# Moving eight of the 32 branch-gate tiles from between the prompt steps into the sampled attention

## What is computed

```python
qa, ka, va, ra, lra, qb, kb, vb, fb, ga, gb = split(h @ w_in)      # ga, gb: (tokens, 2048) each
o_gla = gla_chunked(qa, ka, va, log_a, s0)                         # gated linear attention
# FoX, prompt: causal softmax attention with a forget bias, 8 heads of 128
# FoX, sample: q (4 tokens) against cache_k[page_table], cache_v[page_table], 1024 rows, 8 heads, each of 8 sequences
u_a = (rmsnorm(o_gla) * silu(ra)) @ w_up_a
u_b = o_fox @ w_up_b
merged = sigmoid(ga) * u_a + sigmoid(gb) * u_b
x = x + gt1 * (merged @ w_out)
# then a mixture of experts with 16 experts, and a final norm
```

## Time and profile before

| | us |
|---|---|
| median of 3 runs | 2014.64 |
| lowest and highest | 2011.6 to 2017.98 |
| the profiled execution's own time | 2012.6 |
| its span, first to last instruction | 2011.0 |

### The profile page before, as it was taken

The page is one execution under the profiler, slowest core; times in us unless marked ns, Lnnn a source line. Parts: engine busy times, 40 slices in busy tenths (PEclk is TensorE's granted clock), DMA queues, the critical chain, the costliest instruction groups (busy, mean ns, idle before and its releaser), DMA issues.

```text
span 2011.0 us, 28008 instructions
## 1 busy us (share of the span) xinstructions
PE 1792.2 (89%) x11118; PEld 1123.2 (56%) x11118; DVE 536.1 (27%) x1145; ACT 210.2 (10%) x403; POOL 154.1 (8%) x266
## 2 busy tenths in 40 slices
PE   6589999999998999999667899998699898999998
PEld 3055666666666777777545677776333333333334
DVE  2020000000017643332665311102423322232223
ACT  2010000000001110111223110001200001000102
POOL 1011021111110000150000000000100000000000
PEclk9889999999999999999778899999799999998998
DMA  9997676775705433543799985324299999999991
GB/s 359 420 359 273 238 284 222 266 290 192 272 22 172 156 96 106 179 158 104 297 410 410 365 307 195 119 94 168 68 366 393 408 383 395 409 392 403 369 395 47
DMA packets 142972, 530.89 MB, mean 264 GB/s; under 512 B 17637, under 2 KB 54667, under 8 KB 116123
## 3 DMA queue, kind: packets, MB, share of 16 engines
q1 hardware_dynamic: 117876, 433.50, 56.3%
q0 software_dynamic: 16704, 95.96, 13.6%
q10 hardware_dynamic: 8336, 0.66, 0.3%
HBM read 510.94 MB, written 19.15 MB: 264 GB/s over the span
## 4 chain that ended last, share of the span: by engine, by line
PE 74%; DMA 12%; DVE 5%; issue 4%; SPq 3%; DVEq 1%; ACT 1%; POOLq 0%; POOL 0%; ACTq 0%
PE ps L610 71%; DMA ring<-in_w_up_e_dram 4%; DMA ring<-in_cache_k_dram 3%; DMA ring<-in_w_ada_dram 3%; DMA xT<-in_w_ada_dram 2%; PE ps L620 2%; SPq L377 1%; DVE ring L1701 1%; SPq L383 1%; DVE z L1354 1%; DVE ring L1351 1%; DVE z L1345 1%; DMA z<-in_x_sample_dram 0%; DVEq L1976 0%; DVE ring L1441 0%
## 5 line engine op out<-in xcount | busy, mean ns | idle before, releaser
L610 PE MATMUL ps<-hT,ring 128*128 128x288 f32 x2560 | 649.1, 412 | 8.3 <-ACT hT L1169 6.3
L610 PEld LDWEIGHTS ps<-hT,ring 128*128 128x128 f32 x2560 | 483.5, 192 | 178.6 <-issue 51.1
L610 PE MATMUL ps<-ring,work 128*64 128x512 f32 (+1 forms) x1280 | 279.4, 636 | 37.9 <-DMA ring<-in_w_ada_dram 26.8
L610 PE MATMUL ps<-ring,z 32*32 32x256 f32 (+3 forms) x3744 | 227.5, 438 | 69.3 <-DVE ring L1701 53.4
L610 PE MATMUL ps<-z,ring 128*128 128x288 f32 (+1 forms) x1040 | 257.7, 408 | 5.7 <-PE ps L610 3.1
L1354 DVE COPY z<-ps 128x256 f32<-128x256 f32 (+7 forms) x98 | 64.4, 660 | 708.5 <-PE ps L610 678.2
L610 PEld LDWEIGHTS ps<-z,ring 128*128 128x128 f32 x1040 | 197.6, 191 | 64.0 <-issue 8.0
L610 PEld LDWEIGHTS ps<-ring,z 32*32 32x32 f32 (+3 forms) x3744 | 113.3, 121 | 171.2 <-issue 164.0
L610 PEld LDWEIGHTS ps<-ring,work 128*64 128x64 f32 (+1 forms) x1280 | 78.3, 135 | 204.1 <-issue 163.2
L1169 ACT ACTIVATE z<-ps 128x512 f32<-128x512 f32 (+4 forms) x108 | 60.4, 601 | 923.0 <-PE ps L610 909.2
L1351 DVE SCALAR_TENSOR_TENSOR xT<-ps,modT,xT 128x256 f32<-128x256 f32 x160 | 70.8, 480 | 262.1 <-PE ps L610 262.1
(11 more groups left out here) (200 smaller groups left out, 795.8 us busy)
## 6 DMA issues: line engine op xcount, KB each, us to landing
ring<-in_w_in_dram SPq DMA_DIRECT2D x40, 2048.0 KB, 12.5
xT<-in_w_ada_dram POOLq DMA_DIRECT2D x64, 1024.0 KB, 6.9
ring<-in_w_gate_e_dram SPq DMA_DIRECT2D x32, 2048.0 KB, 13.5
ring<-in_w_up_e_dram SPq DMA_DIRECT2D x32, 2048.0 KB, 18.8
ring<-in_w_down_e_dram SPq DMA_DIRECT2D x32, 2048.0 KB, 15.3
ring<-in_w_ada_dram SPq DMA_DIRECT2D x16, 2048.0 KB, 26.5
ring<-in_cache_k_dram SPq DMA_DIRECT2D x64, 512.0 KB, 6.0
ring<-in_cache_v_dram SPq DMA_DIRECT2D x64, 512.0 KB, 6.9
```

Of the source, the lines that this page charges most:

```text
L610: return nc.tensor.matmul(o, lhsT, rhs, start=start, stop=stop, skip_group_check=free)
```

## The change

Only 24 of the 32 gate tiles (384 of the 512 matmuls) are left between the prompt steps. `gates(n)` is called at the same places with smaller counts. From first to last, with the count before: eight levels 11 (16); 8 (16), 6 (8), 8 (8); 14 (16) after the sampled states' outputs; eight updates 4 (6); 12 (16), 10 (16), 14 (16), 12 (16), 12 (16); in FoX eight times 5 (8) and eight times 2 (4). The counts ahead of the levels stay. ACT's `keep_gates` lists are moved to fit.

The other eight tiles are gate gb's last eight. One is worked in each iteration of the sampled attention, behind `turn_probs(b)`, in PSUM bank 5 (`late_gate`). Its weights, 1 MB in 2,048 runs of 128 floats (512 bytes), go into the residual's buffer, where `r_rep` stood (`late_w`, one buffer). SP issues them between the keys of b + 1 and the values of b, and waits first for ACT's copy of the late tile before. ACT copies the tile to `stage[0]` at the end of its iteration, POOL stores it to DRAM and lets the buffer go. SP also waits for `r_turn_ready` ahead of its loop, and `gates_back(0)`, which overwrites `hT`, goes behind the last values and waits for the last late tile.

```diff
@@ shapes and constants
+        late_w = xflat[:, 2112:2112 + KT * P].rearrange("p (k n) -> p k n", n=P)
-        LATER = 8
+        LATER = 6
@@ sync
-            for m in range(16):
+            for m in range(12):
...
+            def late_gate_weights(b):
+                sp.wait_ge(sem("late_gate_copied"), b + 1)
+                sp.dma_start(late_w, io["w_in"][0, :, ds(b * P + (COL_GB + 8 * P), P)].rearrange("(k p) n -> p k n", p=P)).then_inc(sem("late_gate_full"), 16)
...
+            sp.wait_ge(sem("r_turn_ready"), 1)
             with sp.Fori(0, DB - 1) as b:
                 pages(b + 1, 0)
                 pages(b + 1, 1)
+                late_gate_weights(b)
                 pages(b, 2)
                 pages(b, 3)
...
+            late_gate_weights(DB - 1)
             up_weights(0)
-            for i in range(3):
-                sp.wait_ge(sem(f"gate_kept{i}"), 16 * ((32 - i + 2) // 3))
-            gates_back(0)
             pages(DB - 1, 2)
             pages(DB - 1, 3)
+            for i in range(3):
+                sp.wait_ge(sem(f"gate_kept{i}"), 16 * ((24 - i + 2) // 3))
+            sp.wait_ge(sem("late_gate_copied"), DB + 1)
+            gates_back(0)
...
+                    sp.wait_ge(sem("late_gate_kept"), 16 * DB)
                     gates_back(2)
@@ gpsimd
+            with pool.Fori(0, DB) as b:
+                pool.wait_ge(sem("late_gate_copied"), b + 2)
+                pool.dma_start(gates_kept[:, ds(b * T + 24 * T, T)], stage[0]).then_inc(sem("late_gate_kept"), 16)
+                pool.wait_ge(sem("late_gate_kept"), b * 16 + 16)
+                pool.sem_inc(sem("stage_free"), 1)
@@ tensor: gates(n) between the prompt steps
-                gates(16)
+                gates(11)
...
-            gates(16)
+            gates(8)
...
-                gates(6)
+                gates(4)
...
-                    gates(8)
+                    gates(5)
...
-                    gates(4)
+                    gates(2)
...
-            pe.wait_ge(sem("gate_copied"), 32)
+            pe.wait_ge(sem("gate_copied"), 24)
...
+            def late_gate(b):
+                pe.wait_ge(sem("late_gate_full"), b * 16 + 16)
+                pe.wait_ge(sem("late_gate_copied"), b + 1)
+                for k in range(KT):
+                    last = mm(ps[:, 5, 0:T], late_w[:, k, :], hT[:, k, :], k == 0, k == KT - 1)
+                last.then_inc(sem("late_gate_tile"), 1)
...
                 score(b)
                 weigh_values(b - 1)
                 turn_probs(b)
+                late_gate(b)
...
+            pe.wait_ge(sem("late_gate_copied"), DB + 1)
             for g in range(2):
                 last = tr(ps[:, 5, g * P:(g + 1) * P], o_all[:, g, :])
@@ scalar
-                if n >= 1:
-                    keep_gates(5 + n)
-            keep_gates(12)
+                keep_gates(*((), (6,), (7,), (8,), (), (9,), (10,))[n])
...
-                keep_gates(*((), (26,), (27,), (), (28,), (29,), (30,), (31,))[h])
+                keep_gates(*((), (), (20,), (), (21,), (), (22,), (23,))[h])
...
+                act.wait_ge(sem("late_gate_tile"), b + 1)
+                act.wait_ge(sem("stage_free"), b + 1)
+                f(stage[0], ps[:, 5, 0:T], ACT.Copy).then_inc(sem("late_gate_copied"), 1)
@@ vector
...
             v.drain()
+            v.sem_inc(sem("r_turn_ready"), 1)
             find_max(0)
```

More of the change, by code:

```diff
@@ L384, in pages @@
                                  io[name][0, ds(pg, 1)].rearrange("a p h d -> (a p) (h d)")).then_inc(sem(f"kv_full{s}"), 16)
-            store_gate(28)
-            store_gate(29)
+            def late_gate_weights(b):
+                sp.wait_ge(sem("late_gate_copied"), b + 1)
+                sp.dma_start(late_w, io["w_in"][0, :, ds(b * P + (COL_GB + 8 * P), P)].rearrange("(k p) n -> p k n", p=P)).then_inc(sem("late_gate_full"), 16)
+            store_gate(20)
+            store_gate(21)
             pages(0, 0)
-            store_gate(30)
-            store_gate(31)
+            store_gate(22)
+            store_gate(23)
             pages(0, 1)
+            sp.wait_ge(sem("r_turn_ready"), 1)
             with sp.Fori(0, DB - 1) as b:
@@ L800, in _ @@
             last.then_inc(reach("state1_ready"), 1)
-            gates(8)
+            gates(6)
             pe.wait_ge(*step("state1_copied"))
@@ L826, in _ @@
             last.then_inc(reach("os_state_ready"), 1)
-            gates(16)
+            gates(14)
             for b in range(DB):
@@ L842, in _ @@
             last.then_inc(reach("os_turned"), 1)
-            gates(16)
+            gates(12)
             pe.wait_ge(*step("oa_squared"))
@@ L849, in _ @@
             last.then_inc(reach("ss_a_ready"), 1)
-            gates(16)
+            gates(10)
             pe.wait_ge(*step("rs_a_ready"))
@@ L1234, in _ @@
             f(decay, decay, ACT.Exp).then_inc(reach("decay_exp"), 1)
-            keep_gates(*range(13, 21))
+            keep_gates(*range(11, 16))
             act.wait_ge(*step("oa_copied"))
@@ L1239, in _ @@
             f(sq8, oaT, ACT.Square).then_inc(reach("oa_squared"), 1)
-            keep_gates(21)
+            keep_gates(16)
             act.wait_ge(*step("ms_a_ready"))
@@ L1244, in _ @@
             f(sig8, ra, ACT.Sigmoid).then_inc(reach("ra_sig"), 1)
-            keep_gates(22, 23, 24, 25)
+            keep_gates(17, 18, 19)
             for h in range(H_B):
@@ L1271, in sample_sequence @@
                 f(pTN, ps[0:TS, 4, 0:2 * P].rearrange("p (g t) -> p g t", g=2), ACT.Copy).then_inc(sem("pt_copied"), 1)
+                act.wait_ge(sem("late_gate_tile"), b + 1)
+                act.wait_ge(sem("stage_free"), b + 1)
+                f(stage[0], ps[:, 5, 0:T], ACT.Copy).then_inc(sem("late_gate_copied"), 1)
             act.wait_ge(sem("oa_final"), 1)
+            act.wait_ge(sem("gate_kept0"), 16 * 8)
             with act.Fori(0, DB) as b:
@@ L1360, in _ @@
                             *((f"ring_free{s}", 1) for s in range(SLOTS)),
-                            ("combined_read", 1)):
+                            ("combined_read", 1), ("late_gate_copied", 1), ("stage_free", 1)):
                 v.sem_inc(sem(name), n)
```

## The result

| | before | after |
|---|---|---|
| median of the runs | 2013.38 us (4 runs, 2011.6 to 2017.98) | 1987.99 us (4 runs, 1984.46 to 1991.44) |
| ratio | | 0.9874, 95% interval 0.9855 to 0.9892 |
| profiled execution, own time | 2012.6 | 1988.57 |
| its span | 2011.0 | 1987.0 |

The change is faster, as forecast, but by 25.4 us by the medians and 24.0 by the two spans, where I had written 13.5. The time forecast was 2001, and the measured one stands at the low end of the range, 1988.0, a hundredth of a microsecond outside. So the gain is 20 to 25 us. By either, the forecast gain was too small.

The account below looks back on a forecast made before the run. PE was taken to bound the prompt steps and DMA the sampled attention. 60.6 us saved less 47.1 lost made 13.5 us faster: 1999.1 us profiled, 2001 by the median; range of 8 in 10, 1988 to 2016 us.

Parts of the forecast that it names:

- What bounds what: Between the prompt steps PE is the bound; in the sampled attention DMA is, at a share of 1.03.
- The signs named for the profile: Expected trace: levels 7.1 to 7.3 us apart, FoX ending near 897, keys 24 to 25 apart, first up tile near 1114.
- The matmuls: 128 matmuls leave the prompt steps at 0.493 us each, 63.1 us; outside FoX all were counted as saved.
- FoX: the step that failed: In FoX 8 x (3 + 2) matmuls save 19.7 us, less 2.5 for waits shown, 1.5 in POOL's head.
- The loop: Sampled attention: late weights 3.8 us and store 0.4 per sequence lengthen the period from 20.5 to 24.7; six periods lose 25.2.
- The keys that wait for `r_turn_ready`: The second sequence's keys are issued 4.4 us later (3.7 to 4.9), after DVE's copy, with DMA idle meanwhile.
- The tail: Seventh late tile, last sequence and eighth late tile in a row before up projections: 29.1 us instead of 17.1, 12.0 lost.
- The clock on the first tile: PE's clock, fallen while waiting for weights, lengthens the seventh late tile by 0 to 3.4 us; 1.7 taken.
- Case 2: Late weights in the sampled attention cost only 2.6 us each, line rate at 512 bytes: 1992 us, chance 0.15.
- Case 3: Packets below 1,024 bytes cost 49 ns, 2018 us, or prompt steps wait on DVE, ACT and POOL, 2014; together 0.18.
- Case 4: The late tile makes the loop a chain: PE's clock falls to 1.2 GHz, DMA runs dry; 2030 us, chance 0.12.
- all prompt savings: The prompt's upper bound, 63 us saved with no wait showing; with cheap late weights it gave the low end, 1988 us.

Follow-up runs that it names:

- both halves: Against the kernel before: small counts without late tiles, 1947.2 us (0.967); old counts with the eight late tiles worked again in the loop, 2054.68 us (1.0214).
- e_few_bytes: Changed kernel, but only the first 64 KB of each late tile's 1 MB of weights is fetched; 1967.49 us, ratio 0.9769 to the kernel before.
- both measurements: The changed kernel measured twice, unaltered: 1987.99 us (ratio 0.9874) and later 1991.59 us (0.9896), each against the kernel before.
- e_late_only: Kernel before with its old counts, all 32 gate tiles between prompt steps, plus the last eight worked again in the sampled attention; 2054.68 us, ratio 1.0214.
- e_wait_moved: Changed kernel with SP's wait for `r_turn_ready` moved from ahead of its loop to just before each late-weights issue; 1984.92 us, ratio 0.9856 to the kernel before.

## Why the forecast was right in kind and wrong in size

**What bounds what: right.** PE bounded the prompt and DMA the loop. The share stayed at 1.03 to 1.05, and both halves came out as sums of terms. The signs named for the profile came, but for two: FoX ended at 891.28 and not near 897, and the first up tile stood at 1103.54 and not near 1114.

**The matmuls: right.** 0.493 us each, 43.7 us in the levels, updates and single steps where 43.4 were written.

**FoX: the step that failed.** "I take 2.5 us off" was written for POOL: the head that it disturbs would show 1.5 us more, others some tenths. I carried the collision over from the earlier trace rows as if it belonged to the head. It belonged to a meeting that 1.7 us of delay had brought about, and with shorter heads POOL's instruction fell between two pairs of DVE. In the changed kernel no wait behind POOL was left, where I had expected 3 us. The shorter fillings laid no wait bare in any other head either: PE waited for DVE once in FoX, 1.24 us in the last head, and that wait stood in the kernel before too (before, then after):

```profile
953.37 0.55 PE L620 MATMUL ps<-ident,z 128*128 128x128 f32 x3 [1.25 <-DVEq L1682]
...
888.17 0.55 PE L637 MATMUL ps<-ident,z 128*128 128x128 f32 x3 [1.24 <-DVEq L1711]
```

The first filling's 5.84 us at the lower clock, which stood in the trace of before and in no group of mine, was gone. So instead of 19.7 - 2.5 = 17.2 the term was 22.8, 5.6 us of the 10.5 that I missed. Worse than the value was the bound: I let nothing show at best, which excluded that the change could take away a wait that was there. I bounded that term on one side only.

**The loop: right in mechanism, each term a little large, 4.6 us in all.** Packets of 27.7 ns and not 29.8 with the store at 0.37 us made periods of 24.40 and not 24.7: 1.6 us in six and 0.2 at the first. The keys that wait for `r_turn_ready` cost 3.7 and not 4.4: 0.7. The tail was sized from the first sequence's softmax, 12.4 us, in a stretch where PE was busy for 8.51 of 10 us; the last one's took 1095.78 - 1084.34 = 11.4, and no 0.9 us gap stood before the up tiles. These sum to 13.7 - 11.7 = 2.0. The clock on the first tile was right, 9.64 us instead of 7.9, the 1.7 that I took. (The bound of 3.4 was written without its working; the longest late tile, 10.98 us, was 3.1 over.)

**The cases.** Case 2 (1992 us) gave the measured time for the wrong reason. The late weights did not cost 2.6 us but 3.55, so its condition did not hold, though its time did. The rule of the Trainium skill behind it ("DMA: Bandwidth & Descriptors", Specifications), that 512 bytes already run at line rate, is not borne out here: the same megabyte took 3.55 us in 512-byte runs and 2.44 in 8,192-byte ones. Case 3 fell on both counts: the packet was cheaper than 49 ns, and the prompt gave all of its 63 us. Case 4 fell to the late tiles of 9.7 to 11 us that changed no beat, and to e_few_bytes.

**The range.** 1988 was case 2 "with all prompt savings", though the terms as written make 2001 - 8.6 - 2.5 = 1989.9. So the low end stood about 2 us below its own sum, and that it came within a hundredth of the result is luck. With FoX bounded in both directions, by the 3.3 us of lower clock and collision that the trace of before held, the terms would have reached 1986.6 and the range held both measurements.

## What to carry to other kernels

Work that fills an engine's waits is worth its full price when the filling ends after the answer it covers: count those instructions, times their row, and trust the sum. A wait or a slow instruction that comes from two engines meeting must be treated as a matter of phase. Any edit ahead of it may remove it as well as lengthen it, so it belongs in the range with both signs. And when bytes move into a stage that the DMA engines already fill, ask also which transfer comes last there: issuing the late weights ahead of the keys cost no byte and took 3 us off the end.

## What the chip did that I had not expected

The granted clock fell where PE had hardly been idle. In the kernel before, PE was busy for 8.70 of the nine us ahead, and the clock of the next 4 us was 0.57:

```profile
868.00:877.00 9.00, 8.70 (x38) 6.15 (x37) 3.08 (x11) 1.70 (x2) 4.60 (x7) 1.00 0.68 237
...
877.00:881.00 4.00, 4.00 (x10) 2.90 (x11) 1.00 (x3) 0.92 (x4) 0.96 (x1) 0.57 0.97 288
```

e_late_only had the same numbers in the nine us ahead and kept 1.00 in the four behind them:

```profile
870.70:879.70 9.00, 8.70 (x38) 6.15 (x37) 3.09 (x11) 1.70 (x2) 4.61 (x7) 1.00 0.68 237
...
879.70:883.70 4.00, 4.00 (x18) 3.16 (x18) 1.01 (x3) 0.92 (x4) 0.91 (x1) 1.00 1.02 316
```

I had written that a PE that is never idle isn't given the low clock. These rows contradict it, and I have no cause: the stretch at the lower clock stands in both profiles of the kernel before, at the same place, and in none of the ten of other kernels, where FoX's first filling ran at full clock.

Executions that are the same from the levels on can start them some us apart. DVE's answer ahead of the levels came at 632.66 us in the first profile of before, at 633.16 and 632.87 in the two of the changed kernel, at 638.95 in e_wait_moved, which has the same instructions up to there. For differences of a few us I therefore measured from landmark to landmark.
